# Six single experts and thirteen pairs in another order, nine weight buffers, and two edits at the start of a two-block transformer kernel

## What is computed

```python
mod = (c_act @ ada_w[layer] + ada_b[layer])          # 6 x 1024, scale and shift of both halves, gates
h = modulate(rms_norm(x, attn_norm[layer]), sh_a, sc_a)
mix = diff_attention(h, ...)                         # 8 heads, q, k, v of 128 columns each
...
g_sel = argmax(hf @ w_rg + b_rg)                     # one of 4 groups
top_p, top_i = top_k(softmax(e_logits[g_sel]), 2)    # 2 of its 8 experts
# each of 32 experts, over the tokens that chose it:
hid = silu(xb @ w_gate[e]) * (xb @ w_up[e])          # 1024 -> 512
y = hid @ w_down[e]                                  # 512 -> 1024
x = x + g_f * sum of the two weighted y of a token; then the final norm
```

## Time and profile before

| | |
|---|---|
| median of the runs | 2410.09 us |
| the profiled execution | 2407.38 us |
| its span (first to last instruction) | 2405.6 us |
| TensorE matmuls busy | 2271.1 us (94%) |
| VectorE, ScalarE, GpSimd busy | 1224.5, 511.4, 43.0 us |
| read from and written to HBM | 444.54 and 18.39 MB |
| mean granted TensorE clock | 0.977 |

### The profile page before, as it was taken

The page is one execution under the profiler, slowest core; times in us unless marked ns, Lnnn a source line. Parts: engine busy times, 40 slices in busy tenths (PEclk is TensorE's granted clock), DMA queues, the critical chain, the costliest instruction groups (busy, mean ns, idle before and its releaser), DMA issues. The chain is left out here.

```text
span 2405.6 us, 26715 instructions
## 1 busy us (share of the span) xinstructions
PE 2271.1 (94%) x9870; PEld 1525.0 (63%) x9870; DVE 1224.5 (51%) x2808; ACT 511.4 (21%) x1167; POOL 43.0 (2%) x50
## 2 busy tenths in 40 slices
PE   7899899999999999989999999999999999889886
PEld 4444588888887655558888888845578443333332
DVE  4444477667766256666655667667566111111014
ACT  2223313330002144441333100112232000000001
POOL 0000000000000000000000000000000000001000
PEclk9999999999999999999999999999998999999998
DMA  7544313353532111113443435311034589999995
GB/s 297 223 161 165 133 71 140 141 209 142 201 149 114 62 62 53 43 56 123 174 193 153 198 146 204 141 70 70 1 140 167 203 358 427 426 426 426 423 425 215
DMA packets 45460, 452.73 MB, mean 188 GB/s; under 512 B 7785, under 2 KB 7785, under 8 KB 20241
## 3 DMA queue, kind: packets, MB, share of 16 engines
q1 hardware_dynamic: 37616, 435.64, 45.5%
q0 software_dynamic: 6528, 12.17, 1.4%
q10 hardware_dynamic: 1184, 3.19, 0.3%
HBM read 444.54 MB, written 18.39 MB: 192 GB/s over the span
## 5 line engine op out<-in xcount | busy, mean ns | idle before, releaser
L3003 PE MATMUL ps<-ring,big 128*64 128x512 f32 (+1 forms) x768 | 232.6, 609 | 28.4 <-issue 15.7
L1213 PE MATMUL ps<-big,ring 128*128 128x256 f32 x768 | 186.0, 379 | 0.6 <-PE ps L1128 0.6
L1128 PE MATMUL ps<-hT,ring 128*128 128x256 f32 x768 | 178.3, 381 | 0.0
L3003 PEld LDWEIGHTS ps<-ring,big 128*64 128x64 f32 (+1 forms) x768 | 84.7, 151 | 147.4 <-issue 134.2
L3099 DVE TENSOR_TENSOR big<-big,ps 128x512 f32<-128x512 f32 x20 | 13.8, 688 | 296.1 <-ACT big L3068 282.0
L1128 PEld LDWEIGHTS ps<-hT,ring 128*128 128x128 f32 x768 | 144.8, 190 | 23.2 <-ACT hT L434 4.1
L537 PE MATMUL ps<-hT,ring 128*128 128x512 f32 x336 | 153.9, 608 | 5.8 <-DMA ring<-in_stream 5.8
L1213 PEld LDWEIGHTS ps<-big,ring 128*128 128x128 f32 x768 | 145.6, 190 | 21.0 <-issue 1.4
L2084 PE MATMUL ps<-hT,ring 128*128 128x512 f32 x320 | 142.4, 600 | 2.7 <-DVE big L2466 1.7
L1025 DVE SCALAR_TENSOR_TENSOR ring<-ring,tmp 128x1024 f32<-128x1024 f32 x112 | 136.4, 1219 | 0.0
L3003 PE MATMUL ps<-big 128*64 128x512 f32 (+1 forms) x352 | 128.9, 600 | 7.4 <-ACT big L3064 3.3
(11 more groups left out here) (509 smaller groups left out, 3603.1 us busy)
## 6 DMA issues: line engine op xcount, KB each, us to landing
ring<-in_stream SPq DMA_DIRECT2D x99, 2048.0 KB, 8.7
ring<-in_gate SPq DMA_DIRECT2D x17, 2048.0 KB, 29.7
ring<-in_up SPq DMA_DIRECT2D x16, 2048.0 KB, 26.0
ring<-in_down SPq DMA_DIRECT2D x15, 2048.0 KB, 29.0
big<-in_up SPq DMA_DIRECT2D x9, 2048.0 KB, 24.9
big<-in_down SPq DMA_DIRECT2D x8, 2048.0 KB, 27.9
big<-in_gate SPq DMA_DIRECT2D x7, 2048.0 KB, 26.2
hT<-in_down SPq DMA_DIRECT2D x5, 2048.0 KB, 27.5
```

Source lines behind the costliest of these rows:

```text
L1128: ins = pe.matmul(place(i, name), a[:, k, :], b[:, k, :], start=(k == 0), stop=(k == 3))
L1213: ins = pe.matmul(m.ps[:, bank[name], q * H:(q + 1) * H], a[:, q * P:(q + 1) * P], b, start=(first and q == 0), stop=(final and q == 1))
L3003: ins = pe.matmul(out[a:z, :], left[:, k * P + a:k * P + z], bufs[i % WBUF][:, k * width + c * 512:k * width + (c + 1) * 512], start=(k == ...
```

## The change

1. *Start:* VectorE adds the squared tiles in pairs, and TensorE sums four tiles instead of eight.
2. *Stream of the differential attention:* head 1 comes right after the first modulations (chunk 5 of the stream). The modulation chunks 4 to 11 are worked in heads 1, 2, 3, 3, 4, 5, 5 and 6, none in heads 0 and 7. `modulate` takes a chunk and a tile, and a head's tiles are spread over its four bias steps.
3. *Experts:* six singles and thirteen pairs, 19 blocks. The order is single (pinned), pair, pair, single (pinned), then eleven pairs and four singles spread evenly; in all (F a single, P a pair) F P P F P F P P P F P P P F P P P F P. Up to eleven blocks for the overflow.
4. *Buffers:* nine, and each load goes into the one whose content is used up first. The ninth lies where gathered rows, y and the routing's rows were. Hidden rows, their transposes and gathered rows move into tables that nobody needs any more; load 8 waits in `phase_route` until the routing's rows are picked and written. With the pinned loads first, loads 0 to 2 are those of block 0, 3 to 5 those of block 3, 6 to 8 gate, gate and up of block 1. The y rows are read back into the two buffers that are used up first.
5. The routing's temporary tiles are laid out in another order, `act` waits once for the zero fill of the y rows.

```diff
@@ constants
-OVER = 9
-FULL = 8
+OVER = 11
+FULL = 6
 PAIRS = (EXPERTS - FULL) // 2
 BLOCKS = FULL + PAIRS
-WBUF = 8
+WBUF = 9
@@ phase_start, VectorE
                 dve.tensor_copy(rb[:, 0:512], m.ps[0:16, 0, :]).then_inc(bias_sb, 3)
+                for k in range(0, KT, 2):
+                    dve.wait_ge(sqd, k + 2)
+                    dve.tensor_tensor(m.hT[:, k, :], m.hT[:, k, :], m.hT[:, k + 1, :], ALU.add).then_inc(paired, 1)
                 dve.wait_ge(cond_ok, 1)
@@ phase_start, TensorE
-                for k in range(KT):
-                    pe.wait_ge(sqd, k + 1)
+                for k in range(0, KT, 2):
+                    pe.wait_ge(paired, k // 2 + 1)
                     for j in range(NT):
                         last = pe.matmul(m.ps[:, 3 + j, 0:1], m.hT[:, k, j * P:(j + 1) * P], m.ones[:, 0:1],
-                                         start=(k == 0), stop=(k == KT - 1))
+                                         start=(k == 0), stop=(k == KT - 2))
@@ before phase_diff
+MOD_HEAD = {4: 1, 5: 2, 6: 3, 7: 3, 8: 4, 9: 5, 10: 5, 11: 6}
+
+def diff_order():
+    order = [("head", 0), ("mod", 2), ("mod", 3), ("head", 1)]
+    for h in range(1, DIFF_HEADS - 1):
+        order += [("mod", c) for c in sorted(MOD_HEAD) if MOD_HEAD[c] == h] + [("head", h + 1)]
+    return order
@@ phase_diff
         def weights(h):
-            return at if h == 0 else at + 2 + 2 * h
+            return at + DIFF_ORDER.index(("head", h))
...
-                def modulate(h, j):
-                    n = modulations(h)
+                def modulate(c, j):
+                    n = at + DIFF_ORDER.index(("mod", c))
...
                 for h in range(heads):
+                    own = [(c, j) for c in taken(h) for j in range(4)]
                     for j in range(4):
                         bias(h, 3 - j)
-                        modulate(h, j)
+                        for c, tile in own[j * len(own) // 4:(j + 1) * len(own) // 4]:
+                            modulate(c, tile)
@@ load_order
-    places = [0, 1]
-    for i in range(PAIRS // 2):
-        places += [FULL + 2 * i, PINNED + i, FULL + 2 * i + 1]
+    pairs = list(range(FULL, BLOCKS))
+    fulls = list(range(PINNED, FULL))
+    places = [0, pairs[0], pairs[1], 1]
+    rest = [((i + 0.5) / (len(pairs) - 2), p) for i, p in enumerate(pairs[2:])]
+    rest += [((i + 0.5) / len(fulls), p) for i, p in enumerate(fulls)]
+    places += [p for _, p in sorted(rest)]
@@ new
+def buffer_order():
+    used_up, holds, count = [-1] * WBUF, [None] * WBUF, [0] * WBUF
+    homes = []
+    for i, (kind, t, _) in enumerate(LOADS):
+        j = min(range(WBUF), key=lambda j: (used_up[j], j))
+        count[j] += 1
+        homes.append((j, count[j], holds[j]))
+        used_up[j], holds[j] = STAGES.index((kind, t)), i
+    free = sorted(range(WBUF), key=lambda j: (used_up[j], j))
+    return homes, free[0:2]
@@ weight_buffers
-        m.oT[:].rearrange("p k t -> p (k t)"), m.hT[:].rearrange("p k t -> p (k t)")]
+        m.oT[:].rearrange("p k t -> p (k t)"), m.hT[:].rearrange("p k t -> p (k t)"), m.big[:, 2 * CH:3 * CH]]
@@ phase_route, SyncE
-                    if i == WBUF - 1:
+                    if i == 7:
                         sp.wait_ge(tr, NT)
+                    elif i == 8:
+                        sp.wait_ge(xpick, 2)
+                        sp.wait_ge(m.written, 16 * NT)
                     load_expert(m, sp, i)
@@ phase_experts
-    hid = two(12288, 512)
-    ht = two(13312, 512)
-    y = two(10240, 1024)
+    hid = [m.vec[:, D:D + 512], m.rs[:]]
+    unused = CON["tri_ones"][0] + D
+    ht = [m.zero[:], m.con[:, unused:unused + 512]]
+    y = two(12288, 1024)
...
                 for i in range(WBUF, len(LOADS)):
-                    kind, t, _ = LOADS[i - WBUF]
+                    kind, t, _ = LOADS[HOMES[i][2]]
                     if t or kind == "d":
                         sp.wait_ge(stage[kind], t + 1)
                     load_expert(m, sp, i)
...
                 act.sem_inc(xa, 1)
+                act.wait_ge(m.zfill, 32)
                 gate(0)
@@ gathered_rows
-    return m.big[:, 8192:10240].rearrange("p (s n) -> p s n", s=2)
+    return [m.tmp[:, D:2 * D], m.vec[:, 0:D]]
```

More of the change, by code:

```diff
@@ L444, in diff_rel @@
     return m.big[:, 7424:7424 + 2048].rearrange("p (s m n) -> p s m n", s=2, m=2)
+MOD_HEAD = {4: 1, 5: 2, 6: 3, 7: 3, 8: 4, 9: 5, 10: 5, 11: 6}
[4 more added lines that the diff above has]
+    return order
+DIFF_ORDER = diff_order()
 def phase_diff(nc, m):
@@ L484, in weights, with taken @@
         def weights(h):
-            return at if h == 0 else at + 2 + 2 * h
-        def modulations(h):
-            return at + 3 + 2 * h
+            return at + DIFF_ORDER.index(("head", h))
+        def taken(h):
+            return [c for c in range(4, 12) if MOD_HEAD[c] == h]
         with nc.Block(no_gpsimd_drain=True) as block:
@@ L714, in first_rows @@
                     scale_rows(m, dve, outs, hs, (2 * c, 2 * c + 1))
-                def modulate(h, j):
-                    n = modulations(h)
+                def modulate(c, j):
+                    n = at + DIFF_ORDER.index(("mod", c))
                     if j == 0:
                         dve.wait_ge(m.full[n % RING], 16 * (n // RING + 1))
-                    o = 16 + 4 * h + j
+                    o = 4 * c + j
                     modulation_tile(m, dve, n, j, crow, m.mod0[:, o:o + 1]).then_inc(mod_done, 1)
                     if j == 3:
-                        dve.wait_ge(mod_done, 8 + 4 * (h + 1))
+                        dve.wait_ge(mod_done, 4 * (c - 1))
                         dve.sem_inc(m.free[n % RING], 1)
@@ L753, in _ @@
                     dve.tensor_copy(aT[:, koff[1]:koff[1] + width[1]], m.ps[:, landing[1], 0:width[1]]).then_inc(tr_d, 1)
-                dve.wait_ge(mod_done, 8 + 4 * heads)
+                dve.wait_ge(mod_done, 40)
                 dve.tensor_tensor(m.mod0[:, 16:48], m.mod0[:, 16:48], fl(m, "ada_b0")[:, 16:48], ALU.add)
@@ L2623, in load_order @@
     pinned = [x for x in loads if x[2] < PINNED]
-    return places, pinned + [x for x in loads if x[2] >= PINNED]
+    return places, pinned + [x for x in loads if x[2] >= PINNED], stages
 def ranks_of(place):
     return [place] if place < FULL else [2 * place - FULL, 2 * place - FULL + 1]
-PLACES, LOADS = load_order()
+PLACES, LOADS, STAGES = load_order()
+def buffer_order():
[8 more added lines that the diff above has]
+    return homes, free[0:2]
+HOMES, FREE = buffer_order()
 def weight_buffers(m):
     return [m.big[:, 0:CH], m.big[:, CH:2 * CH]] + [m.ring[:, (N_STREAM + j) % RING, :] for j in range(RING)] + [
-        m.oT[:].rearrange("p k t -> p (k t)"), m.hT[:].rearrange("p k t -> p (k t)")]
+        m.oT[:].rearrange("p k t -> p (k t)"), m.hT[:].rearrange("p k t -> p (k t)"), m.big[:, 2 * CH:3 * CH]]
 def load_expert(m, sp, i):
@@ L2646, in load_expert @@
     w = {"g": m.d_gate, "u": m.d_up, "d": m.d_down}[kind]
-    sp.dma_start(weight_buffers(m)[i % WBUF], w[bass.ds(e, 1), :, :].rearrange("o p n -> p (o n)")
-                 ).then_inc(m.wfull[i % WBUF], 16)
+    j = HOMES[i][0]
+    sp.dma_start(weight_buffers(m)[j], w[bass.ds(e, 1), :, :].rearrange("o p n -> p (o n)")).then_inc(m.wfull[j], 16)
 def expert_rows(m):
@@ L2666, in take @@
         return s[:, at[0] - n:at[0]]
+    cmp = take(OVER * EXPERTS).rearrange("p (b e) -> p b e", b=OVER)
+    bex = take(OVER)
+    incl = take(EXPERTS)
     lg3 = take(NT * 36).rearrange("p (i n) -> p i n", i=NT)
@@ L2676, in phase_route @@
     sc = take(NT * 8).rearrange("p (j i) -> p j i", j=8)
-    cnt, over, start, tmp32, incl, key, rank, base, cap, jump, less, more, at_rank = (take(EXPERTS) for _ in range(13))
+    cnt, over, start, tmp32, key, rank, base, cap, jump, less, more, at_rank = (take(EXPERTS) for _ in range(12))
     key_rows, rank_rows = take(1), take(1)
@@ L2681, in phase_route @@
     nbc = take(2)
-    cmp = take(OVER * EXPERTS).rearrange("p (b e) -> p b e", b=OVER)
-    bex = take(OVER)
     assert at[0] <= 2048
@@ L2945, in phase_experts @@
     last = BLOCKS - 1
-    yrows = [bufs[j].rearrange("p (i n) -> p i n", i=NT) for j in range(2)]
+    yrows = [bufs[j].rearrange("p (i n) -> p i n", i=NT) for j in FREE]
     with Phase(nc) as ph:
@@ L3019, in front @@
                         for i in weights(kind, t):
-                            pe.wait_ge(m.wfull[i % WBUF], 16 * (i // WBUF + 1))
+                            pe.wait_ge(m.wfull[HOMES[i][0]], 16 * HOMES[i][1])
                         for k in range(KT):
@@ L3041, in down @@
                     for k in range(4):
-                        ins = product("d", t, [m.ps[:, 6, :], m.ps[:, 7, :]], ht[:, s, :], k, D)
+                        ins = product("d", t, [m.ps[:, 6, :], m.ps[:, 7, :]], ht[s], k, D)
                     ins.then_inc(dn, 1)
@@ L3167, in final_gain @@
 def final_gain(m):
-    return m.big[:, 8192 + D * ((BLOCKS - 2) % 2):8192 + D * ((BLOCKS - 2) % 2) + D]
```

(3 more changed lines are left out.)

23 lines of the change are left out of this document (11 added, 12 removed).

## The result

The changed kernel takes **2369.77 us** (median of 4 runs, 2366.88 to 2375.61), the kernel before 2410.42 (4 runs, 2404.18 to 2411.45). The ratio is 0.9844, 95% interval 0.9828 to 0.9860: 1.6% faster. 2369 was predicted, with a range of 2355 to 2384 and a chance of 0.94 for faster.

What follows compares the result with a forecast made beforehand. TensorE was taken to set the pace up to about 1,880 us, weight transfers in the expert stage; 14 us from start and attention plus 25.5 from the experts, 39.5 in all, gave 2369 us, range 2355 to 2384.

Steps and rivals of the forecast that it cites:

- The hole: DMA gap in the expert stage's first 60 us: load 13 would start 29 us earlier, bounds 20 and 32.
- Rival 1: Expert stage's beginning: transfers still stall, half the hole remains, gain 10 to 12 us, result 2383; chance 0.10.
- The saved block: Expert stage: one block fewer saves about 24 us of TensorE alone, covered by the DMA bound, costed at nothing.
- The tail, +3.5 us: End of expert stage: read back stands behind the last weights until 2343.5, charged 3.5 us, bounds 0 and 7.8.
- The start, 5 us,: Sum of squares and first projection: paired adds let the projection end at 54.5 to 55; 5 us gained, bounds 2 and 6.
- The stream, 8 us,: Differential attention: head 1's weights land earlier, removing TensorE's 5.80 us wait and slow restart; 8 us gained.
- Rival 2: Start gains nothing, DMA-bound, or heads 3 and 5 get longer; 5 to 6 of 14 us left, 2377; chance 0.08.
- Head 7, +1 us,: Attention's head 7 loses its last modulation tile ahead of the reciprocal: 1 us gained, 0 to 2.
- rival 3: Expert stage: longer waits for weights drop TensorE to its lower clock, making it slower, up to 2550; chance 0.05.
- rival 4: Experts: with six singles, blocks go into the overflow code, eleven serial blocks, 2800 us; chance 0.01.

Runs made afterwards that it cites:

- end_pairs: Changed kernel with the blocks behind the fourth spread otherwise, ending in two pairs instead of a single and a pair; median 2369.5 us, ratio 0.9838.
- stream_only: Kernel before with only the stream of the differential attention changed, start and experts as before; median 2409.3 us, ratio 0.9995.

## Why the prediction was right, step by step

**The hole.** Predicted 29 us (20 to 32), measured 29.6 up to the last product that waits for weights. The releases came in the predicted order. In times of the kernel before (add 2.1 us to the new ones) SyncE issues at 1893.6, 1900.5, 1908.9 and 1917.7, where the working has 1892.6, 1899.7, 1908.5 and 1917.3. The hole that is left, some 3 us before 1892, was put at 2.5. Rival 1, half the hole staying, is refuted by the windows at 0.97 to 1.01. What the working couldn't tell apart is now priced: the choice of buffers about 12.6 us, the ninth buffer about 6.7, the order of the first blocks 8.5, and the saved block 2.2. The choice of buffers was measured by adding it to the old kernel, the others by taking them one at a time from the whole, so these are shares in one order of counting; that they add up to 30.0 is partly luck, as each is known to some 3 us only.

**The saved block at nothing.** 2.2 us in the stage, not clear of the spread, so the claim of a cover holds: the DMA bound lies just below TensorE's. Fewer blocks than nineteen should bring nothing more (argued, not run).

**The tail, +3.5 us.** This term was mis-sized. The last transfer ahead of the read back (the final gain, behind all weights) is issued at 2307.28 and lands 33.9 us later, at 2341.2; forecast were 2343.5 less 2.1. The read back is issued at 2336.09 and lies beside it. SyncE's timeline and two windows of the changed kernel:

```profile
2307.28 0.43 SPq L3017 DMA_DIRECT2D vec<-in_final  x1
2336.09 4.05 SPq L3023 DMA_DIRECT2D ring<-expert_rows  x8
```
```profile
2320.00:2330.00 10.00, 8.73 (x39) 3.98 (x39) 2.01 (x3) 0.60 (x1) 0.99 (x1) 1.00 0.74 311
2330.00:2340.00 10.00, 9.22 (x45) 3.47 (x41) 0.69 (x1) 0.60 (x1) 0.00 (x0) 1.00 0.57 217
```

The read back took 8.91 us instead of 7.80, +1.1. The working had the moments right and took the DMA for full until the last load lands; but the 16 engines were busy 0.74 and then 0.57 of the last 20 us, so the read back had room beside it. And the down product at 2283.25 runs at full clock, 7.09 instead of 8.64, -1.5 us, which the working had not counted. Sum: -0.4 (90.25 against 90.6) instead of +3.5. That such a term exists end_pairs shows, with a read back of 13.64 us. The Trainium skill, "DMA: Bandwidth & Descriptors", section "Issuing engines are not separate DMA queues", has DMAs of SyncE and GpSimd interleave on the same 16 engines whichever of them started them. The trace agrees in kind: the read back lands beside the last loads and takes 1.1 us more, the scatter of GpSimd 10.62 us instead of 10.41.

**The start, 5 us,** came as 4.6 at the first projection's start and 4.9 at its end (59.53 to 54.66), and nothing of the adds is seen: the last ends at 18.90, the first modulation starts at 19.18 when its chunk lands. **The stream, 8 us,** came as 13.1 - 4.9 = 8.2 at head 1. In the medians it isn't seen: stream_only gains 0.05%, with an interval from 5 us faster to 2 us slower. No head is longer than 28.93; the eight modulation tiles of heads 3 and 5 are free, and the slots' margins of 6 to 7 us hold. Rival 2 is refuted at its places.

**Head 7, +1 us,** is wrong. It took 22.6 us to the spread instead of 21.9, so -0.6, and the spread behind it another 2.7. The working counted VectorE's queue and left out that TensorE can be at its lower level behind idle times (granted clock 0.55 in the spread instead of 1.00), although rival 3 had the mechanism for the experts. The step that failed is a silent one, a loss put at nothing without a reason: that a gain at head 1 goes through 1,800 us of other phases undiminished. Medians give 7 to 12 us for the front instead of 14; where the rest goes stays open.

**The clock in the experts' stage (rival 3)** didn't come: 0.98 in the window shown. Single products behind a wait are slow as before: the up product at 2272.10, behind 2.60 us of idle time, takes 8.75 us instead of 7.09, and costs nothing there, since the down product waits for its own weights until 2283.25 anyhow. The Trainium skill, "TensorE: Matmul & The Clock Gate", section "HAM oscillation", has a product start cold again behind each wait for the next weights. The trace agrees in kind, with 1.7 us at such a wait, and not in weight: the products here, 21 us a block, are far longer than the waits. **The overflow (rival 4)** isn't seen: nineteen blocks, then the end.

**The sum** was right in part by luck: the stage gained 30.0 where 25.5 were forecast, the front 2.1 in the profiled executions and 7 to 12 in the medians where 14 were. By the medians the whole is 40.6 us, predicted 39.5. Two errors of some 4 us cancel.

## What to carry to other kernels

When a stage is bound by transfers, look for the one hole at its beginning: what is closed there comes out whole at the end, since everything behind keeps its rate (29.6 us earlier at the last product that waits for weights, 30.0 at the end of the stage). Buffers in fixed rotation hold a load back for the slowest user; give each load the buffer that is used up first, put blocks that free two buffers a stage early, and one buffer more is worth one transfer. A gain far ahead of the end should be discounted: here 7 to 12 of 13 us arrived. And where two profiles of the same code differ by 6 us at a mark, more than one pair is needed before a loss is given a place.

## What the runs showed that I had not expected

- Two profiled executions of one kernel agreed within 0.4 us at every mark, and both were 6 us longer than its other runs (2375.6 and 2376.2 against 2366.9 to 2370.0; clock 0.968 and 0.966 against 0.975 and 0.976). A difference of two profiles below 6 us says nothing on the medians. Seven profiles with the same code up to the routing's end put it up to 6.8 us apart.
- The same 32 matmuls took 3.81, 5.43 or 6.53 us, and with the same idle times to 0.02 us ahead of them 3.81 in two profiles and 5.43 in a third.
- A block less was worth 2.2 us, within the spread, where TensorE's share of it is 24.1.
- An earlier end of the last but one block by 6.7 us (end_pairs) brought 1.0, since the read back beside the last loads took 13.64 us instead of 8.91.
